# Recurrent input units first, the others as filling; the sparse selection in quarters; one table for exp and ln

## The reference, cut to what matters

```python
def mixer_block(x, w_in, ...):                      # first block, each layer
    p_swa, p_rwkv, p_fox, p_dsa, p_gate = split_cols(x @ w_in, IN_GROUPS)
    o_swa = swa_branch(...)                         # window attention with sinks
    o_rwkv = rwkv7_branch(p_rwkv, mu, ...)          # recurrence over tokens
    o_fox = fox_branch(...)                         # attention with a forget bias
    o_dsa = dsa_branch(...)                         # attention on the 64 best keys of an index score
    gates = sigmoid(p_gate.reshape(B, S, 4, D) + gate_bias)
    merged = sum_i gates[:, :, i] * (o_i @ w_i)
    return merged @ w_out
# x = layer_norm(ALPHA * x + mixer); then a dense FFN (layer 0) or 8 experts, top 2 (layer 1)
# second block, each layer: modulated RMS norm, 4 pairs of block attention heads and
# 4 differential heads, each head's q, k and output RMS-normalised, out projection, FFN
```

## Time and profile before

| | |
|---|---|
| median of 3 runs | 2380.99 us (2380.73 to 2382.38) |
| profiled execution | 2379.34 us, span 2377.6 us |
| TensorE busy, weight loads | 2177.4 us (92%), 1566.2 us |
| VectorE, ScalarE, GpSimd busy | 654.0, 435.2, 81.7 us |
| mean granted TensorE clock | 0.954 of full |
| HBM read | 417.90 MB, 176 GB/s over the span |
| first block, layer 0 | mixer until about 430 us, FFN until 675 us |
| first block, layer 1 | mixer until about 1115 us, experts until 1550 us |
| second block | 1550 to 1965 us and 1965 to 2377 us |

### The profile page before, as it was taken

How to read it: one execution, slowest core, us unless ns; L and a number is a source line. 1 busy time by engine, 2 the same in 40 slices (tenths; PEclk the granted TensorE clock), 3 DMA queues, 4 the chain that set the end, 5 groups by cost and what they waited for, 6 DMA issues and landing times.

```text
span 2377.6 us, 34188 instructions
## 1 busy us (share of the span) xinstructions
PE 2177.4 (92%) x14812; PEld 1566.2 (66%) x14812; DVE 654.0 (28%) x1567; ACT 435.2 (18%) x897; POOL 81.7 (3%) x180
## 2 busy tenths in 40 slices
PE   8999679999989897788899999988899998889998
PEld 7878457677768686565554365367577766757775
DVE  0051643424320333643200000033433332341001
ACT  0031131100010121230000000046610004661000
POOL 2000000001000000001000000000001010000000
PEclk9999869999999899788899999999999999999999
DMA  8333203488744232112899999953368854232442
GB/s 252 110 107 108 98 18 115 160 265 292 251 148 138 89 107 98 53 63 91 265 345 333 360 346 310 375 185 104 110 209 269 296 185 135 91 105 91 159 159 88
DMA packets 329659, 421.25 MB, mean 177 GB/s; under 512 B 21015, under 2 KB 277989, under 8 KB 329509
## 3 DMA queue, kind: packets, MB, share of 16 engines
q1 hardware_dynamic: 308304, 352.96, 46.0%
q0 software_dynamic: 13408, 50.66, 6.3%
q10 hardware_dynamic: 7796, 15.43, 1.9%
HBM read 417.90 MB, written 1.05 MB: 176 GB/s over the span
## 4 chain that ended last, share of the span: by engine, by line
PE 46%; ACT 4%; DVE 4%; issue 1%; DMA 1%; ACTq 0%; DVEq 0%
PE psum L1219 11%; PE psum L1336 10%; PE psum L1237 6%; PE psum L1396 5%; PE psum L1226 5%; PE psum L1635 2%; PE psum L1878 1%; PE psum L1255 1%; PE psum L1464 1%; PE psum L1325 1%; PE psum L1409 1%; ACT arena L996 1%; PE psum L1155 1%; ACT L967 1%; PE psum L1618 1%
## 5 line engine op out<-in xcount | busy, mean ns | idle before, releaser
L1219 PE MATMUL psum<-xT,ring 128*128 128x256 f32 (+1 forms) x3584 | 801.4, 384 | 7.0 <-DVEq L417 2.9
L1219 PEld LDWEIGHTS psum<-xT,ring 128*128 128x128 f32 (+1 forms) x3584 | 678.5, 190 | 129.5 <-issue 23.0
L1237 PE MATMUL psum<-ring,arena 128*128 128x512 f32 x528 | 232.2, 593 | 0.0
L1226 PE MATMUL psum<-ring,xT 128*128 128x256 f32 (+3 forms) x1024 | 216.8, 370 | 15.5 <-DVE arena L2268 8.1
L1226 PEld LDWEIGHTS psum<-ring,xT 128*128 128x128 f32 x1024 | 185.7, 199 | 44.6 <-DVE arena L2268 9.3
L1237 PEld LDWEIGHTS psum<-ring,arena 128*128 128x128 f32 x528 | 100.0, 190 | 114.2 <-issue 111.9
L2063 DVE TENSOR_TENSOR arena<-arena,psum 128x512 f32<-128x512 f32 x33 | 22.7, 688 | 410.7 <-PE psum L1219 235.0
L2052 DVE SCALAR_TENSOR_TENSOR arena<-arena,cond 128x256 f32<-128x256 f32 x336 | 135.0, 480 | 0.0
L1336 PE MATMUL psum<-ring,arena 128*32 128x256 f32 x2304 | 126.8, 379 | 0.7 <-DVE arena L2135 0.7
L657 ACT ACTIVATE arena<-psum 128x512 f32<-128x512 f32 x33 | 19.7, 597 | 578.2 <-PE psum L1219 571.9
L1336 PEld LDWEIGHTS psum<-ring,arena 128*32 128x32 f32 x2304 | 74.7, 110 | 51.2 <-issue 3.4
(11 more groups left out here) (392 smaller groups left out, 1972.8 us busy)
## 6 DMA issues: line engine op xcount, KB each, us to landing
ring<-in_w_in SPq DMA_DIRECT2D x80, 1024.0 KB, 5.3
ring<-in_exp_w SPq DMA_DIRECT2D x312, 256.0 KB, 6.1
arena<-in_w_mod POOLq DMA_DIRECT2D x48, 1024.0 KB, 9.4
ring<-in_ffn_w SPq DMA_DIRECT2D x33, 1024.0 KB, 6.8
arena<-in_exp_w SPq DMA_DIRECT2D x120, 256.0 KB, 7.1
ring<-in_w_gate SPq DMA_DIRECT2D x22, 1024.0 KB, 7.6
ring<-in_w_up SPq DMA_DIRECT2D x22, 1024.0 KB, 10.0
ring<-in_w_down SPq DMA_DIRECT2D x22, 1024.0 KB, 5.1
```

Source lines behind the costliest of these rows:

```text
L1219: ins = pe.matmul(dst, w[:, k * 256 + c0:k * 256 + c0 + m], act_t[:, k, :], start=(k == 0), stop=(k == KT - 1))
L1226: ins = pe.matmul(dst, act_t[:, k, t * P:t * P + P], w[:, k * 256 + c0:k * 256 + c0 + n], start=(k == 0), stop=(k == KT - 1))
L1237: ins = pe.matmul(psum[:, 4 + 2 * t + h, :], gT[:, s % 3, f * 256 + t * P:f * 256 + t * P + P], w2[:, f * D + h * 512:f * D + h * 512 + 51 ...
```

## The change

1. The recurrence's input units (3 to 6) come first. The other nine join the 16 gate units in one list of 25 (`FILL_IN`, `fill` in place of `gates`): 10, 11, 12, 7, 8, 9, 0, 1, 2, then the gates. ScalarE copies all of them out. The barrier behind the input units goes; VectorE waits for the constants, the parameters and the copies it needs.
2. `G` distributes them anew: three (layer 0) or two (layer 1) before the up-projections, the same places in the recurrence, one behind the variance of the normalisation, one or two (`in_attention`) before attention, and one for each of the i = 0 to 8 in attention.
3. Unit 11's columns are packed anew: sparse k and index k side by side in one channel tile of 128, and v, index weights and forget logits in token tiles of 72 columns. The forget logits thus come by token and are transposed on TensorE at the start of the attention stage.
4. The selection rounds move from in front of `attention` into it, in quarters (`choose`) behind the masks of units 0 to 3.
5. In the second block ScalarE loads `natural_log_exp_and_others`, a table with both functions, once per layer before `keep_rows`. VectorE refines each inverse root by one Newton step (`newton`, three operations).

The other lines of the diff rename, or move the index scores to a buffer for each block of queries.

```diff
+RWKV_IN = (3, 4, 5, 6)
+FILL_IN = (10, 11, 12, 7, 8, 9, 0, 1, 2)
+FILLS = len(FILL_IN) + 16
...
+        RAW_BANK = {3: 4, 4: 5, 5: 0, 6: 1}
+        PAR_BANK = 2
...
-                for i, c in enumerate(units1):
+                for i in RWKV_IN + FILL_IN:
+                    c = units1[i]
                     if c is None:
-                        yield ("in", l, i), [(0, 128, w[:, :, IN_DSA + 256:IN_DSA + 384]),
-                                             (128, 68, w[:, :, IN_DSA + 640:IN_DSA + 708]),
+                        yield ("in", l, i), [(0, 64, w[:, :, IN_DSA + 256:IN_DSA + 320]),
+                                             (64, 64, w[:, :, IN_DSA + 640:IN_DSA + 704]),
+                                             (128, 64, w[:, :, IN_DSA + 320:IN_DSA + 384]),
+                                             (192, 4, w[:, :, IN_DSA + 704:IN_DSA + 708]),
...
+            def fill(l, n, banks):
 
                 for _ in range(n):
-                    j = gates_done[0] % 16
-                    gates_done[0] += 1
-                    cp, b = gate_place(j)
-                    act.wait_ge(*ready("pe_job", "gate", l, j))
-                    for i in range(2):
-                        c = 2 * cp + i
-                        step(act.activation(zb[:, b, c, :], psum[:, banks[j % len(banks)], i * 256:i * 256 + 256],
-                                            ACT.Identity, bias=prm(l, "gate_b", b * KT + c)), "zb", l, j)
-
-            gates_done = [0]
+                    j = filled[0] % FILLS
+                    filled[0] += 1
+                    bank = psum[:, banks[j % len(banks)], :]
+                    act.wait_ge(*ready("pe_job", "fill", l, j))
+                    if j >= len(FILL_IN):
+                        cp, b = gate_place(j - len(FILL_IN))
+                        for i in range(2):
+                            c = 2 * cp + i
+                            step(act.activation(zb[:, b, c, :], bank[:, i * 256:i * 256 + 256],
+                                                ACT.Identity, bias=prm(l, "gate_b", b * KT + c)), "filled", l, j)
+                    elif FILL_IN[j] == 2:
+                        for g in range(2):
+                            for h in range(2):
+                                step(act.copy(swa_k[hb(h), g, :], bank[hb(g), 0:256]))
+                        step(act.copy(swa_v[:], two(bank[:, 256:512])), "filled", l, j)
+                    elif FILL_IN[j] == 11:
+                        for h in range(2):
+                            step(act.copy(dsa_k[hb(h), :], bank[0:HD, 0:256]))
+                            step(act.copy(dsa_ki[hb(h), :], bank[HD:P, 0:256]))
+                        token = bank[:, 256:400].rearrange("p (t c) -> p t c", t=NT)
+                        step(act.copy(dsa_v[:], token[:, :, 0:HD]))
+                        step(act.activation(dsa_wi[:], token[:, :, HD:HD + 4], ACT.Copy, scale=SCALE * 0.5))
+                        step(act.copy(forget, token[:, :, HD + 4:HD + 8]), "filled", l, j)
+                    else:
+                        dst = {0: swa_q[:, 0:2, :], 1: swa_q[:, 2:4, :], 7: fox_q, 8: fox_k, 9: fox_v,
+                               10: dsa_q, 12: dsa_qi}[FILL_IN[j]]
+                        step(act.copy(dst[:], two(bank)), "filled", l, j)
+
+            filled = [0]
...
+                for i, dst in ((3, raw[:, 0:2, 1:]), (5, raw[:, 4:6, 1:])):
                     act.wait_ge(*ready("pe_job", "in", l, i))
-                    step(act.copy(dst, psum[:, in_bank(i), :].rearrange("p (a b) -> p a b", a=2)), "in", l, i)
+                    step(act.copy(dst, two(psum[:, RAW_BANK[i], :])), "in", l, i)
...
-                barrier()
-
-                gates(l, G[0], (6,))
+                fill(l, G[0][l] - 1, (6,))
                 act.wait_ge(*ready("dve", "mix", l))
...
+                fill(l, in_attention(l), (0, 1))
...
+                act.wait_ge(*ready("act", "filled", l, FILLS - 1))
...
+                act.preload_act_table_set("natural_log_exp_and_others")
...
+                    key = ("in", l, FILL_IN[j]) if j < len(FILL_IN) else ("gate", l, *gate_place(j - len(FILL_IN)))
+                    w = unit(*key)
+                    if key == ("in", l, 9):
+                        for t in range(NT):
+                            ins = token_tile(psum[:, bank, t * 256:t * 256 + 256], w, 0, 256, t)
+                    elif key in (("in", l, 2), ("in", l, 11)):
+                        n_tok = P if key[2] == 2 else HD + 8
+                        channel_tile(psum[:, bank, 0:256], w, 0, P)
+                        for t in range(NT):
+                            ins = token_tile(psum[:, bank, 256 + t * n_tok:256 + (t + 1) * n_tok], w, P, n_tok, t)
+                    else:
+                        for i in range(2):
+                            ins = channel_tile(psum[:, bank, i * 256:i * 256 + 256], w, i * P, P)
+                    job(ins, "fill", l, j)
+                    used(*key)
+                    fill_in[bank] = j
+
+            filled, fill_in = [0], {}
 
...
+                fill_in.clear()
+                fill(l, 1, (6,))
...
+                    turn_mod(0, PAR_BANK)
+                fill(l, G[0][l] - 1, (6,))
...
-                gate_in.clear()
+                fill_in.clear()
+                for t in range(NT):
+                    ins = pe.transpose(psum[0:4, 2, t * P:t * P + P], forget[:, t, :], ident[:])
+                job(ins, "forget", l)
 
...
+            def choose(qt, half):
+
+                k0, nk = KEYS[qt]
+                rounds_of = TOPK // 16
+                for rnd in range(rounds_of * half, rounds_of * (half + 1)):
+                    src = picked[:, (rnd - 1) % 2, 0:nk] if rnd else score[:, qt, 0:nk]
+                    step(dve.max(m8, src))
+                    step(dve.match_replace(picked[:, rnd % 2, 0:nk], m8, src, TAKEN))
+                if half:
+                    left = picked[:, (TOPK // 8 - 1) % 2, 0:nk]
+                    step(dve.tensor_tensor(part[:, 0:nk], left, score[:, qt, 0:nk], ALU.is_equal))
+                    step(dve.tensor_scalar(dsa_bias[:, k0:k0 + nk], part[:, 0:nk], NEG, None, ALU.mult))
+
             def attention(l):
                 n = len(UNITS1)
                 for i in range(n + 4):
                     if i < n:
                         scores_in(l, i, UNITS1[i])
+                    if i < 4:
+                        choose(i // 2, i % 2)
                     if i >= 4:
                         outs(l, i - 4, UNITS1[i - 4])
                     if 1 <= i < n + 1:
...
+            def newton(r, s, scale, add):
+
+                t = refine[:, 0:s.shape[1]]
+                step(dve.scalar_tensor_tensor(out=t, in0=r, scalar=-0.5 * scale, in1=r, op0=ALU.mult, op1=ALU.mult))
+                step(dve.scalar_tensor_tensor(out=t, in0=s, scalar=add, in1=t, op0=ALU.add, op1=ALU.mult))
+                step(dve.scalar_tensor_tensor(out=r, in0=t, scalar=1.5, in1=r, op0=ALU.add, op1=ALU.mult))
+
...
+                newton(ri8[:, b], ss8[:, b], 1.0, RMS_EPS)
...
+                newton(ro4[:, b, 0:m], os4[:, b, 0:m], 1.0 / d, 0.0)
...
+                for i in (4, 6):
...
+                    step(dve.tensor_copy(raw[:, i - 2 if i == 4 else i:(i - 2 if i == 4 else i) + 2, 1:],
+                                         two(psum[:, RAW_BANK[i], :])), "in", l, i)
+                if l == 0:
+                    dve.wait_ge(*ready("pool", "constants"))
+                    dve.wait_ge(*ready("act", "par"))
+                else:
+                    mod_columns(0, PAR_BANK)
+                    dve.wait_ge(*ready("act", "in", l, 5))
 
                 step(dve.tensor_tensor(mix[:], raw[:, :, 0:SEQ], raw[:, :, 1:], ALU.subtract))
...
+                dve.wait_ge(*ready("pe_job", "forget", l))
+                step(dve.tensor_scalar(fox_t[low, 0, :], psum[0:4, 2, 0:SEQ], fbias[:, l:l + 1], None, ALU.add))
...
-G = [2, 1, 1, 1, (1, 1, 1, 1, 0), (1, 1, 0, 0), 2, (4,), 1, 0, 1]
-assert G[0] + G[1] + G[2] + G[3] + sum(G[4]) + sum(G[5]) + G[6] + len(G[7]) + G[8] + G[9] + G[10] == 16
-BARRIERS_1 = 4
+G = [(3, 2), 1, 1, 1, (1, 1, 1, 1, 0), (1, 1, 0, 0), None, (0, 1, 2, 3, 4, 5, 6, 7, 8), 1, 1, 1]
+
+
+def in_attention(l):
+    return FILLS - (G[0][l] + G[1] + G[2] + G[3] + sum(G[4]) + sum(G[5]) + len(G[7]) + G[8] + G[9] + G[10])
+
+
+BARRIERS_1 = 3
```

More of the change, by code:

```diff
@@ L220, in build @@
         fox_t = view(4, SEQ)
-        score, picked, part = view(SEQ), view(NT, SEQ), view(SEQ)
+        score, picked, part = view(NT, SEQ), view(2, SEQ), view(SEQ)
         dsa_bias = view(PACK)
@@ L266, in build @@
         m8 = small[:, 144:152]
+        refine = small[:, 112:120]
         ss16, rt16, ri16 = [small[:, 152 + 16 * i:168 + 16 * i] for i in range(3)]
         lam = small[:, 200:208]
+        forget = small[:, 120:128].rearrange("p (t h) -> p t h", t=NT)
         cf = small[:, 160:164].rearrange("p (b q) -> p b q", b=2)
@@ L761, in attention @@
                     if i in G[7]:
```

(38 more changed lines are left out.)

123 lines of the change are left out of this document (24 added, 99 removed).

## The result

The changed kernel takes 2258.19 us (median of 4 runs, 2256.21 to 2261.39) beside 2381.68 us before (4 runs): a ratio of 0.9482, 95% interval 0.9466 to 0.9499. A second series gave 0.9474 (0.9461 to 0.9486). The forecast was 2249 us, range 2226 to 2290: the result lies inside, 9 us above the forecast and 1 us above its own range of 2236 to 2257. The profiled execution took 2261.39 us, the slowest of its four, at a span of 2259.6.

The account below looks back on a forecast made before the run. TensorE was taken as the bound engine, its gains less work, fewer idle stretches or a higher clock. Terms -27.2 - 7.3 - 12.4 - 55.3 - 29.8 = -132.0 us from 2379.34 gave 2247.3, median 2249 us; range 2226 to 2290.

Parts of the forecast that it names:

- its own range: The total time if the forecast itself, not a rival, holds: 2236 to 2257 us, chance 0.62.
- Part 1: Unit 11, first block: repacked, it takes 8.0 us instead of 21.10 and 23.10; with added forget transposes, -27.2 us.
- step 3: Trace table's row for the stretch behind the normalisation, forget transposes included: forecast -12.4 us.
- Part 2: Start of the first block's recurrence: barrier and idle time before the up-projection go, layer 1's recurrence speeds up; -7.3 us.
- the 5.8 us that layer 1 was to win in the recurrence: Layer 1's recurrence took 140.40 us instead of 134.58, behind unit 11's narrow tiles; this excess was to go.
- Part 3: Behind the first block's normalisation: one fill of 6.96 us goes into the 11.81 us stretch; -6.2 a layer, -12.4 us.
- Part 4: First block's attention: fills between score pairs, selection in quarters hidden beside them; 117.3 and 120.1 us long, -55.3 us.
- The allowance for the slow clock: First block's attention: 3.5 us for each of two forgetting units, rounded up to 10 us for the stage.
- Rival (a): First block's attention keeps its clock of 0.73 to 0.8; up to 23 us a layer, 2265 to 2295; chance 0.14.
- rival (b): VectorE bounds attention's first units, or ScalarE's queued fill copies hold the single bank; 18 us, 2257 to 2270; chance 0.08.
- Part 5: Second block: one table removes 64 loads from ScalarE, VectorE gets three operations in each place; -29.8 us.
- the 4.4 us wait: Second block: TensorE's longest wait, where pairs queue on ScalarE; its disappearance was a sign of the forecast being right.

Follow-up runs that it names:

- the experiment gave 8.5: The changed kernel with the fill behind the normalisation's variance moved to the head of attention: 2266.7 us, ratio 0.9524.
- The two experiments: Changed kernel with all four selection quarters before attention's first score: 2282.17 us; changed kernel with each attention stage's nine fills in front of it: 2320.05 us.
- the medians of the experiment: The changed kernel without the early table load and the refinement on VectorE in the second block: 2277.17 us, ratio 0.9563.

## Why the prediction came out as it did

**Part 1** was right within 2.5 us. A 72-column record took 0.115 us; the forecast took 0.14, with 0.22 as its dear bound. Its sum holds 1 us for the forget transposes, which the table books under step 3: like for like it is 28.2 against 29.7, and 11.4 against 11.2 in step 3.

**Part 2**: the first up-projection came at 67.76 us against 68 forecast, the 2 us wait for unit 11's copies was 2.06, the parameters held TensorE for 0.4 us. Mis-sized was the 5.8 us that layer 1 was to win in the recurrence: 2.4 from the up-projection to the variance, 3.2 before it.

**Part 3** was right: 11.2 for 12.4, and the experiment gave 8.5 for the 8.6 expected of it. That close a match is luck, for the stages lost 11.8 and other stretches gave 3.3 back.

**Part 4** was right in mechanism and 4.6 us too careful: 112.84 and 118.54 us for 117.3 and 120.1. (These windows differ by 6.0; 1.4 of it was lost again before the branch matmuls.) The idle 4.1 us before the first score were 3.8. The allowance for the slow clock, 10 us a layer, is what was too large: mean clocks of 0.94 and 0.93 over these lengths are, by an estimate, 6.8 and 8.3 us. The two experiments bear out that the quarters need the fills beside them. Rival (a), a clock of 0.73 to 0.8, is out at 0.94; rival (b) did not occur, though its queue is real and showed when VectorE was late.

**Part 5** is the step that was mis-sized: 29.8 forecast, 23 in the stages of both pairs of traces, and 19 between the medians of the experiment. Of the 6.8 us that are missing, 5.5 are waits: 4.3 and 8.7 us of idle time are left in the stages where 1.9 and 5.6 were allowed. The sentence that failed is that a chain shortens by more "where pairs queue on ScalarE, as before TensorE's longest wait of 4.4 us", with only a copy of 0.7 us left. Two loads went, and the wait fell to 2.21, for the copy stands behind the square and the head sums as well, and I had not written down that chain. In layer 0 the slow clock behind it stayed too: TensorE's records there took 133.47 us instead of 133.87, where -2.6 was hung on the vanished waits. In layer 1 they took 126.36 instead of 131.89, a little more than the -4.7. Putting the copy first shows both at once, 1.3 us of wait in each layer, and 3.2 and 1.6 us of clock. That the 4.4 us wait would be gone was wrong. In layer 1 the first wait is 4.41 us where 3.7 were worked out. What held: no load is left between logarithm and exponential, and without the three operations the median is the same.

**What the sum left out.** 11.9 us were lost in stretches whose instructions are the same. The windows of the branch matmuls in both layers, layer 1's output rows and the first feed-forward in the changed kernel:

```profile
318.12:355.76 37.64, 34.80 (x161) 30.32 (x161) 19.95 (x32) 8.80 (x10) 0.00 (x0) 0.99 0.08 26
944.69:984.02 39.33, 36.49 (x161) 31.51 (x161) 19.91 (x32) 8.81 (x10) 0.00 (x0) 0.95 0.07 22
984.02:1014.59 30.57, 30.57 (x64) 13.30 (x65) 5.60 (x8) 0.47 (x2) 11.46 (x29) 0.90 0.35 90
384.74:631.17 246.43, 236.94 (x1009) 173.98 (x1008) 96.94 (x249) 15.26 (x26) 18.44 (x21) 0.99 0.69 229
```

and the same kernel's branch matmuls and feed-forward in its second profile:

```profile
325.53:364.86 39.33, 36.49 (x161) 31.50 (x161) 19.95 (x32) 8.35 (x10) 0.00 (x0) 0.96 0.05 19
950.69:988.33 37.64, 34.80 (x161) 30.32 (x161) 19.96 (x32) 9.01 (x11) 0.00 (x0) 0.99 0.08 25
392.43:638.87 246.44, 236.94 (x1009) 173.98 (x1008) 96.95 (x249) 15.26 (x26) 18.44 (x21) 0.99 0.69 229
```

The branch matmuls take 37.64 or 39.33 us, and whether one layer, both or neither gets the longer one changes from one profile to the next; the output rows took 27.57 to 30.65 us over the 13 profiles of this case. The profile of before had drawn 37.64, 37.65, 27.57 and 27.57, the best of each; the other twelve lie 3.1 to 7.8 us above that in sum, the changed kernel's own two 6.1 and 3.2. So some 3 us are chance from one profile of the same kernel to the next. That the rest is chance too is likely and not shown, for there is one profile of before; its execution was 2.3 us faster than the median of its kernel. The feed-forward looks different: 244.5 to 246.5 us in all the changed profiles, 242.92 before. In it TensorE waits 3.0 us instead of 1.2 for VectorE's products with the modulation's weights (168 of them, over 201.2 us instead of 199.3), whose transfers take 10.1 us instead of 9.4 at the median of the whole run. Why they are slower was not tested; with unit 11 alone the stretch took 244.20. It stays open. The other 2.5 us of the 11.9 lie in the experts (439.8 for 439.1) and between the two attention stages of the second block (265.2 for 263.4).

The two traces are 2.1 + 11.9 = 14.0 us above the forecast's own terms; the median is only 9 above the forecast, because the profiled run was 3.2 us slower than the median of its kernel, and that of before 1.65 faster than the median that the forecast used.

## What to carry to other kernels

A wait that waits for several things is booked on the last to end. Before a gain is hung on removing what it names, write down for each of the others when it would be done without it; here another chain ended 0.03 us apart. Work that fills gaps and work that is cut into pieces for those gaps belong to one sum: undoing the pieces cost 24 us, undoing the gaps' filling 62. And a forecast made from one profile inherits that profile's luck in stretches that it never mentions; a look at how such stretches differ from layer to layer gives its size.

## What the runs showed of the chip that was not expected

In layer 0 of the second block, a wait of 2.21 us was followed by 61 records at a mean clock of 0.78 in that window, and one of 0.92 us at the same place by none below 1.00: 1.3 us of waiting were worth 4.5. In layer 1 the same 2.21 us went with a clock of 0.88 and were worth 2.9, and in one profile with a clock of 1.00, so that only the waiting itself was lost. At this one place the wait thus cost either nothing beyond itself, or 1.6 or 3.2 us more. Many waits cost more clock: the fills in front left 24.6 us of waits in a stretch of 73.7, and its clock was 0.58, lower than the 0.73 of the earlier trace rows.

The times of unchanged stretches come in steps and not as a scatter: the branch matmuls 37.64 or 39.33 us, the output rows 27.57, 29.0 or 30.6.
